# Gate products of a gated recurrence: three single-pass products with halves made by GpSimd, in place of one four-pass product with a VectorE copy

## The chip, the cores and the metric

One NeuronCore of one Trainium2 chip runs the whole program. The time is the device time of one execution in microseconds (us), the median of several runs. Engines are named as in the profile: PE is TensorE's matmul side, PEld its weight load, DVE is VectorE, ACT is ScalarE, POOL is GpSimd, SP is SyncE (it issues most DMAs). SBUF is the on-chip memory of the engines, PSUM the accumulators that PE writes.

## The reference, cut to what matters

One layer of a decoder for 256 prompt tokens and 64 sample tokens (8 sequences of 8), width 1024, all in fp32:

```python
proj = x @ w_in + b_in                                # 1024 -> 7 x 1024: xa, ga, b_gate, c_gate, v, m_a, m_b
xa_c = causal_dwconv(xa, ...)  + conv_a_b             # width 4
r = sigmoid(blockdiag(wa) xa_c + ba)                  # 16 heads of 64 x 64: the gate products
i = sigmoid(blockdiag(wx) xa_c + bx)
a = exp(-8 r softplus(-lam));  b = sqrt(1 - a^2) * (i * xa_c)
h = scan(h = a h + b)
y_a = h * gelu(ga);  y_b = b_gate * causal_dwconv(c_gate * v, ...)
x = layernorm(alpha x + (sigmoid(m_a) y_a + sigmoid(m_b) y_b) @ w_out)
x = layernorm(alpha x + moe_ffn(x))                   # 32 experts, 4 of them for each token, fp32 weights
```

The change touches the two gate products (`r` and `i`) alone.

## The kernel before, in words

**Stages.** First the projection: 8 blocks c of 128 channels, each with 7 pieces of `w_in` (xa, c_gate, v, ga, b_gate, m_a, m_b, called j = 0 to 6; q = 7c + j counts them to 55). Then the product with `w_out`, layer norm and routing, then 32 experts (with a few extra rounds), whose weights SP streams through a ring of 11 slots of 2 MB. This stream of some 400 MB begins to fill slots when the projection is over: a slot is loaded when PE has signalled that its last content was read, and the first slots when `proj_done`, `block_ok`, `first_free`, `wout_done` and the end of the layer norm say so.

**A piece of the projection.** SP loads `raw` (128 x 8 x 128 fp32, 512 KB). ACT writes its high half `w_hi` (L484, type fp32r, which PE multiplies in one pass), DVE writes `w_lo = raw - w_hi` (L1067, called from `split_low(q)`, signal `lo_ok`), and PE does 24 matmuls of 128 x 320 (L712): w_hi x_hi, w_hi x_lo, w_lo x_hi for each of 8 slices of the inner dimension. PE may begin piece q when `lo_ok` is q + 1 and ACT has taken the PSUM bank. There are four buffers each of raw, w_hi and w_lo.

**Order on DVE, written out by hand.** In block c DVE does: the copy of the two 128 x 128 gate weights of the block, `wab` to `wcur` (L1139); a copy of conv state (L1142); `w_lo` of j = 4; the convolution of xa into `xc` (L1145, L1146, then six L1110), which signals `xc_ok`; three small copies (L1153 to L1156); `w_lo` of j = 5; the products and the convolution of c_gate v (L1159 to L1167); `w_lo` of j = 6 and of the next block's j = 0, 1, 2; then the work on the gates, which begins with what ACT made of them, has `w_lo` of the next block's j = 3 in its midst, a reciprocal (L1187) and the scan (L1196), and ends with `mixT` (L1200). After most steps DVE waits for its own semaphore (`link`).

**The gates.** After piece j = 6 PE waits for `wcur_ok`, `xc_ok` and the two PSUM banks, and does two products (L722), one with each 128 x 128 weight, of plain fp32 with 320 columns. ACT takes both results (L534, L536), applies tanh (L539), loads a table and takes a square root (L541), and then makes the w_hi of the next block's j = 3.

```python
pe.wait_ge(wcur_ok, c + 1); pe.wait_ge(xc_ok, c + 1); pe.wait_ge(gates_taken, 2 * c + 2)
for a in range(2):
    mm(PS[:, 6 + a, 0:T], wcur[:, a, :], xc, start=True, stop=True).then_inc(gates_done, 1)
```

**POOL** makes constants at the start, zeroes `wab` (its blocks off the diagonal; SP loads the rest behind that), and does nothing after 4 us. `wab` lies in rows 0 and 1 of `x1`, and row 2 holds the raw state rows until PE has turned them (`st_turned`).

Of the kernel before, what the change touches and what calls it, by code (L numbers as in the profile page):

```python
# [13 lines left out]
P = 128  # L14
D = 1024
KC = D // P
SEQ, DB, DS = 256, 8, 8
NS = DB * DS
T = SEQ + NS
# [26 lines left out]
ALU = mybir.AluOpType  # L46
ACT = mybir.ActivationFunctionType
AX_X = mybir.AxisListType.X
F32 = mybir.dt.float32
F32R = mybir.dt.float32r  # L50
I32 = mybir.dt.int32
U32 = mybir.dt.uint32
ds = bass.ds
# [25 lines left out]
def hybrid_layer(nc, x_prompt, x_sample, state_h, state_conv, state_sc, w_in, b_in, conv_a_w,  # L79
# [5 lines left out]
    with ctx:  # L85
# [3 lines left out]
        def sem(name):  # L89
            return ctx.enter_context(nc.semaphore(name))  # L90
# [5 lines left out]
        slot = 4 * WIDE  # L96
        XT, X1 = SLOTS * slot, SLOTS * slot + 12 * D
# [4 lines left out]
        def place(name, shape, offset, dt=F32):  # L102
            return nc.alloc_sbuf_tensor_at(name, shape, dt, offset=base + offset)
# [37 lines left out]
        wab = x1[:, 0:2, :].rearrange("p a (c n) -> p a c n", c=KC)  # L141
# [38 lines left out]
        PS = ctx.enter_context(nc.psum_tensor("PS", [P, 8, HALF], F32))  # L180


        tiles = place("tiles", [P, 12 * T + 2 * P], 5 * slot)
        bgt, cgt, vt, gel, tma, tmb, xc, tr, ti, rr, aa, sq = (tiles[:, i * T:(i + 1) * T] for i in range(12))
        wcur = tiles[:, 12 * T:12 * T + 2 * P].rearrange("p (a n) -> p a n", a=2)
        hh = vt
        uc = cgt
        xa_p, xa_s = xa_pad[:, 0:259], xa_pad[:, 259:347].rearrange("p (b s) -> p b s", b=DB)
# [33 lines left out]
        def route(n):  # L222
# [17 lines left out]
        prm_in, st_in, wab_in, misc_in, ln_in = (sem(n) for n in  # L240
                                                 ("prm_in", "st_in", "wab_in", "misc_in", "ln_in"))
# [8 lines left out]
        x_turned, prm_turned, st_turned = sem("x_turned"), sem("prm_turned"), sem("st_turned")  # L250
        proj_done, proj_taken = sem("proj_done"), sem("proj_taken")
        gates_done, gates_taken = sem("gates_done"), sem("gates_taken")
        wcur_ok = sem("wcur_ok")
        prm_ok = sem("prm_ok")
        xa_free, cv_free, xc_ok, block_ok = sem("xa_free"), sem("cv_free"), sem("xc_ok"), sem("block_ok")
        t_ok, sq_ok = sem("t_ok"), sem("sq_ok")
# [202 lines left out]
        def _(pool):  # L459
# [13 lines left out]
            pool.iota(row_no[:, :], pattern=[[0, 1]], base=0, channel_multiplier=1,  # L473
                      allow_small_or_imprecise_dtypes=True).then_inc(const_ok, 1)


        @block.scalar
        def _(act):
# [25 lines left out]
            for q in range(NP):  # L504
                c, j = q // 7, q % 7
# [45 lines left out]
                act.activation(xT[:, :, t0:t0 + n], src, ACT.Copy).then_inc(x1T_ok, 1)  # L551


            act.wait_ge(wcur_ok, KC)
            act.wait_ge(block_ok, HALF_K + 1)
            for t in range(2):
                act.activation(mix_s[:, t, 0], mix_of(t), ACT.Copy).then_inc(mixhi_ok, 1)
# [6 lines left out]
            for q, t in enumerate(T_ORDER):  # L564
                n = TILES[t][1]
# [5 lines left out]
            t0, n = TILES[T_ORDER[2]]  # L571
# [75 lines left out]
            for q, (t, _) in enumerate(LAST_SUMS):  # L647
                n = TILES[t][1]
# [11 lines left out]
        def _(pe):  # L660
            mm = pe.matmul
# [29 lines left out]
            def turn_rows():  # L691

                pe.wait_ge(prm_in, 112)
                pe.transpose(PS[:, 6, 0:BIN], vrows[0:BIN, 0, :], ident[0:BIN, 0:BIN])
                pe.transpose(PS[:, 6, BIN:NPRM], vrows[0:7 * KC, 1, :], ident[0:7 * KC, 0:7 * KC])\
                  .then_inc(prm_turned, 1)
                pe.wait_ge(st_in, 48)
                for k in range(KC):
                    last = pe.transpose(PS[:, 7, k * 48:(k + 1) * 48], st_rows[0:48, k * P:(k + 1) * P],
                                        ident[0:48, 0:48])  # L700
                last.then_inc(st_turned, 1)

            for q in range(NP):
                c, j = q // 7, q % 7
                pe.wait_ge(lo_ok, q + 1)
                if q > 0:
                    pe.wait_ge(proj_taken, 7 * c + {0: 8, 6: 9}.get(j, j + 2))
                for k in range(KC):
                    if q == 0:
                        pe.wait_ge(xlo_ok, k + 1)  # L710
                    for n, (w, x) in enumerate(((w_hi, x_hi), (w_hi, x_lo), (w_lo, x_hi))):
                        last = mm(PS[:, j % 6, 0:T], w[:, q % RING, k, :], x[:, k, :],  # L712
                                  start=(k == 0 and n == 0), stop=(k == KC - 1 and n == 2))
                last.then_inc(proj_done, 1)
                if q == 0:
                    turn_rows()
                if j == 6:
                    pe.wait_ge(wcur_ok, c + 1)
                    pe.wait_ge(xc_ok, c + 1)
                    pe.wait_ge(gates_taken, 2 * c + 2)  # L720
                    for a in range(2):
                        mm(PS[:, 6 + a, 0:T], wcur[:, a, :], xc, start=True, stop=True).then_inc(gates_done, 1)  # L722

# [1 line left out]
            def project(t, a, ks):  # L727

                t0, n = TILES[t]
                out = PS[64 * a:64 * a + n, 4, :] if t == 2 else PS[0:n, 2 * t + a, :]  # L730
                first, final = {2: (0, KC - 1), 0: (HALF_K, -1), 1: (-1, KC - 1)}[t]
                for k in ks:
                    last = mm(out, mixT[:, k, t0:t0 + n], out_rows(k // 2)[:, k % 2, a * HALF:(a + 1) * HALF],  # L733
                              start=(k == first), stop=(k == final))
                return last
# [11 lines left out]
            for k in range(KC - 1):  # L747
                pe.wait_ge(block_ok, k + 2)
                pe.wait_ge(wout_in[k // 2], 16)
                for a in range(2):  # L750
                    last = project(2, a, [k])
# [4 lines left out]
            for a in range(2):  # L756
                last = project(2, a, [KC - 1])
# [7 lines left out]
            for a in range(2):  # L765
                last = project_split(1, a)
# [41 lines left out]
            for k in range(KC):  # L808
                last = pe.transpose(PS[0:54, 6 + k // 4, (k % 4) * P:(k % 4 + 1) * P], so[:, k, :], ident[:, :])
# [6 lines left out]
               start=False, stop=False)  # L816
            mm(PS[:, 5, 2 * NE:3 * NE], ones_r[:, :], mask[:, 0, :], start=False, stop=True).then_inc(rank_done, 1)
            for t in range(3):
                last = mm(PS[:, 4, 3 * NE:4 * NE], ones_r[:, :], mask[:, t, :], start=(t == 0), stop=(t == 2))
# [186 lines left out]
            i, n, twice = NE - 1, UNITS * (NE - 2), 2 * n_more  # L1006
# [27 lines left out]
            for u in range(2):  # L1034
                w = ring[:, (n + 10 + u) % SLOTS, :]
                for half in range(2):
                    pe.wait_ge(last_in[2 * u + half], 16)
                    last = down(w, hT_last, u, (2 * half, 2 * half + 1), 1)
# [9 lines left out]
            for a in range(2):  # L1048
                pe.wait_ge(ylo_ok, 2 * n_more + (NE + a))
                for t, bank in LAST_SUMS:  # L1050
                    t0, n = TILES[t]
                    last = mm(PS[0:n, bank + a, :], onehotT[:, 1, t0:t0 + n], ys[:, a, :], start=True, stop=True)
# [5 lines left out]
        def _(dve):  # L1058
# [50 lines left out]
            def stt(out, in0, scalar, in1, op0, op1):  # L1109
                return dve.scalar_tensor_tensor(out=out, in0=in0, scalar=scalar, in1=in1, op0=op0, op1=op1)  # L1110
# [6 lines left out]
                part = bias4[rows, c - 1, :]  # L1117
                return dve.tensor_tensor(part, bias_raw[rows, (c - 1) * HALF:c * HALF], part.bitcast(F32), ALU.subtract)

            dve.wait_ge(wab_in, 64)  # L1120
            for c in range(KC):
                def ahead(j):
                    if 7 * c + j < NP:
# [11 lines left out]
                def by_seq(ap, j):  # L1135
                    return ap.rearrange("p (b j) -> p b j", j=j)


                dve.tensor_copy(wcur[:, :, :], wab[:, :, ds(c, 1), :].rearrange("p a c n -> p (a c) n"))\  # L1139
                   .then_inc(wcur_ok, 1)  # L1140

                link(dve.tensor_copy(xa_s[:, :, 0:3], by_seq(state(8, 24), 3)))  # L1142
                ahead(4)
# [3 lines left out]
                for j in range(1, 4):  # L1147
                    stt(pr(xc), xa_p[:, j:j + SEQ], par(CAW + 8 * j, c), pr(xc), ALU.mult, ALU.add)
                    last = stt(sm(xc), xa_s[:, :, j:j + DS], par(CAW + 8 * j, c), sm(xc), ALU.mult, ALU.add)
# [32 lines left out]
                if 1 <= c <= 3:  # L1182
                    last = bias_low(c, 1)
# [57 lines left out]
            for q, t in enumerate(T_ORDER):  # L1241
                n = TILES[t][1]
# [29 lines left out]
            for q, t in enumerate(T_ORDER):  # L1272
                n = TILES[t][1]
# [6 lines left out]
                last = dve.tensor_tensor(mask[:, t, :], left[:, t, 0:NE], lg[:, t, 0:NE], ALU.is_gt)  # L1280
# [28 lines left out]
            for h in range(2):  # L1309
                last = dve.tensor_copy(pos4[:, :, h, 0, :], posm[:, :, :])  # L1310
# [139 lines left out]
            for q, (t, bank) in enumerate(LAST_SUMS):  # L1450
                n = TILES[t][1]
# [5 lines left out]
            for q, (t, _) in enumerate(LAST_SUMS):  # L1457
                n = TILES[t][1]
# [4 lines left out]
                last = stt(x1[0:n, t, :], y_acc[0:n, t, :], mean[0:n, t:t + 1], ln2g[0:n, :], ALU.add, ALU.mult)  # L1463
# [7 lines left out]
            for q, (t, _) in enumerate(LAST_SUMS):  # L1471
                n = TILES[t][1]
# [27 lines left out]
```

## Time and profile before

| | |
|---|---|
| Time, median of 3 runs | 1194.76 us (1194.38 to 1196.05) |
| The profiled execution | 1195.21 us, span of its instructions 1193.4 us |
| Granted clock of TensorE, mean over the span | 0.992 of full speed |
| PE busy | 1144.0 us (96%) |
| DVE busy | 520.1 us (44%) |
| ACT busy | 259.5 us (22%) |
| POOL busy | 3.3 us, 13 instructions |
| The 8 blocks of the projection | from 12 to 222 us of the span |
| Expert stage | from about 271 us to the end |
| DMA in the expert stage | 424 to 429 GB/s in all slices of the page from 328 us to 1163 us |

Times in the text are positions in the span unless they are called durations. A group of instructions has one row with its count (x4 is four records); a plain fp32 matmul of the gates shows as two records. In the timelines and the chain the first number is the start, the second the duration, both in us. A number in square brackets is idle time of the engine before that instruction, with what ended it. The records of successive matmuls overlap, so the distance between starts, not the duration of one, is what a matmul costs. The chain that ended last goes back from the last instruction to what released each step, so what stands in it set the end of the span.

### The profile page before, as it was taken

To read this page: it belongs to the slowest core of one execution; us is meant where nothing else is said; L and a number is where in the kernel's file an instruction comes from. 1 tells how busy PE (TensorE), PEld (TensorE's weight loads), DVE (VectorE), ACT (ScalarE), POOL (GpSimd) and SP (SyncE) were. 2 spreads that over 40 slices of the span, in tenths; PEclk is the share of its full clock that TensorE was granted. 3 is DMA by queue.
4 is the path that set the end of the run, shared out by engine and by line. 5 is a ranking of instruction groups with operands and counts; after the bars stand their busy time and mean duration, and the time that the engine had idled before them with its cause. 6 is when DMAs were issued, how large, how long until landed. Compare 5 with 4: busy or idle time off the path is not lost.

```text
span 1193.4 us, 13950 instructions
## 1 busy us (share of the span) xinstructions
PE 1144.0 (96%) x5682; PEld 555.5 (47%) x5682; DVE 520.1 (44%) x989; ACT 259.5 (22%) x405; POOL 3.3 (0%) x13
## 2 busy tenths in 40 slices
PE   9999999999999999999999989999999999999994
PEld 8999999663333333333333323333333333333331
DVE  6788788882333222333223332322222222222236
ACT  4655655411111111111111111111111111111112
POOL 1000000000000000000000000000000000000000
PEclk9999999999999999999999999999999999999998
DMA  9866964768999999999999999999999999999994
GB/s 235 256 208 176 265 192 132 289 258 331 416 424 427 428 427 427 428 428 428 427 427 428 428 426 427 428 427 428 427 428 429 426 426 428 429 427 427 426 426 158
DMA packets 93420, 443.77 MB, mean 372 GB/s; under 512 B 7864, under 2 KB 65352, under 8 KB 68014
## 3 DMA queue, kind: packets, MB, share of 16 engines
q1 hardware_dynamic: 93182, 442.41, 92.1%
q8 instruction: 45, 0.74, 0.3%
q10 hardware_dynamic: 176, 0.48, 0.1%
q14 instruction: 17, 0.14, 0.0%
HBM read 441.34 MB, written 1.53 MB: 371 GB/s over the span
## 4 chain that ended last, share of the span: by engine, by line
PE 66%; DMA 24%; DVE 7%; ACT 2%; issue 1%; DVEq 0%; SPq 0%; ACTq 0%
PE PS L921 25%; DMA ring<-in_w_gu 19%; PE PS L961 13%; PE PS L712 10%; PE PS L829 6%; DMA ring<-in_w_down 4%; PE PS L851 3%; PE PS L733 2%; PE PS L837 1%; DVE w_lo L1067 1%; DVE tiles L1110 1%; PE PS L844 1%; PE PS L884 1%; PE PS L743 1%; PE PS L1001 1%
## 5 line engine op out<-in xcount | busy, mean ns | idle before, releaser
L921 PE MATMUL PS<-ring,mid 128*64 128x512 f32 x1920 | 422.0, 593 | 20.7 <-DMA ring<-in_w_gu 20.2
L921 PEld LDWEIGHTS PS<-ring,mid 128*64 128x64 f32 x1920 | 135.8, 137 | 300.1 <-issue 257.9
L961 PE MATMUL PS<-ring,mid 128*64 128x512 f32 x960 | 213.1, 596 | 0.0
L1389 DVE TENSOR_SCALAR PS<-PS 128x512 f32<-128x512 f32 x30 | 21.0, 699 | 353.5 <-PE PS L921 353.5
L712 PE MATMUL PS<-x_hi,w_hi 128*128 128x320 f32 x448 | 141.1, 315 | 1.1 <-ACT tiles L530 0.5
L712 PE MATMUL PS<-x_lo,w_hi 128*128 128x320 f32 x448 | 138.9, 310 | 0.0
L712 PE MATMUL PS<-x_hi,w_lo 128*128 128x320 f32 x448 | 138.9, 310 | 0.0
L1371 DVE TENSOR_TENSOR ys<-PS,ys 64x512 fp32r<-64x512 f32 x64 | 44.1, 689 | 193.9 <-ACT ys L617 185.5
L961 PEld LDWEIGHTS PS<-ring,mid 128*64 128x64 f32 x960 | 66.1, 137 | 130.1 <-issue 130.0
L1110 DVE SCALAR_TENSOR_TENSOR x_tok<-PS,gate,x_tok 128x1024 f32<-128x1024 f32 (+1 forms) x93 | 115.0, 1276 | 20.9 <-PE PS L851 20.9
L608 ACT ACTIVATE mid<-PS 128x512 f32<-128x512 f32 x30 | 17.9, 597 | 419.1 <-DVE PS L1389 419.1
L829 PE MATMUL PS<-x,onehot 128*64 128x512 f32 (+1 forms) x396 | 98.7, 617 | 2.9 <-DVE esel L1288 2.9
L712 PEld LDWEIGHTS PS<-x_hi,w_hi 128*128 128x128 f32 x448 | 84.6, 189 | 4.2 <-DVE w_lo L1067 3.5
L712 PEld LDWEIGHTS PS<-x_lo,w_hi 128*128 128x128 f32 x448 | 84.5, 189 | 0.3
L712 PEld LDWEIGHTS PS<-x_hi,w_lo 128*128 128x128 f32 x448 | 84.5, 189 | 0.0
L617 ACT ACTIVATE ys<-PS 64x512 fp32r<-64x512 f32 x60 | 35.5, 591 | 209.2 <-PE PS L961 208.5
L1067 DVE TENSOR_TENSOR w_lo<-raw,w_hi 128x1024 fp32r<-128x1024 f32 x56 | 67.2, 1222 | 19.5 <-ACT w_hi L484 18.9
L851 PE MATMUL PS<-ys,onehotT 128*128 128x512 f32 (+1 forms) x186 | 64.8, 431 | 0.0
L484 ACT ACTIVATE w_hi<-raw 128x1024 fp32r<-128x1024 f32 x56 | 59.1, 1055 | 18.5 <-DMA raw<-in_w_in 18.4
L829 PEld LDWEIGHTS PS<-x,onehot 128*64 128x64 f32 (+1 forms) x396 | 22.8, 136 | 56.0 <-issue 52.3
L851 PEld LDWEIGHTS PS<-ys,onehotT 128*128 128x128 f32 (+1 forms) x186 | 25.5, 176 | 25.4 <-issue 25.2
L585 ACT ACTIVATE mid<-PS 128x512 f32<-128x512 f32 x33 | 19.7, 597 | 67.6 <-PE PS L829 67.6
(241 smaller groups left out, 750.6 us busy)
## 6 DMA issues: line engine op xcount, KB each, us to landing
ring<-in_w_gu SPq DMA_DIRECT2D x125, 2048.0 KB, 41.9
ring<-in_w_down SPq DMA_DIRECT2D x61, 2048.0 KB, 40.2
raw<-in_w_in SPq DMA_DIRECT2D x56, 512.0 KB, 5.9
ring<-in_w_gu SPq DMA_DIRECT2D x6, 1024.0 KB, 8.6
ring<-in_w_down SPq DMA_DIRECT2D x6, 1024.0 KB, 40.1
ring<-in_w_out SPq DMA_DIRECT2D x4, 1024.0 KB, 5.0
x_tok<-in_x_prompt SPq DMA_DIRECT2D x2, 512.0 KB, 5.2
out<-x SPq DMA_DIRECT2D x2, 512.0 KB, 2.7
```

The lines of the kernel that those rows point to most:

```text
L484: act.activation(w_hi[:, q % RING], raw[:, q % RING], ACT.Copy).then_inc(hi_ok, 1)
L617: act.activation(y_rows(a, 0), PS[64 * a:64 * a + 64, XB, :], ACT.Copy).then_inc(yhi_ok, 1)
L712: last = mm(PS[:, j % 6, 0:T], w[:, q % RING, k, :], x[:, k, :], start=(k == 0 and n == 0), stop=(k == KC - 1 and n == 2))
L733: last = mm(out, mixT[:, k, t0:t0 + n], out_rows(k // 2)[:, k % 2, a * HALF:(a + 1) * HALF], start=(k == first), stop=(k == final))
L829: last = mm(PS[64 * a:64 * a + 64, XB, :], onehot[0:n, t, :], x1[0:n, t, a * HALF:(a + 1) * HALF], start=(t == 0), stop=(t == 2))
L851: last = mm(PS[0:n, bank + a, :], onehotT[:, par, t0:t0 + n], ys[:, a, :], start=True, stop=True)
L921: last = mm(PS[64 * a:64 * a + 64, b, :], xgT[:, 2 * (u % 2) + j, u // 2, :], w[:, o:o + HALF], start=False, stop=(u == 3 and j == 1))
L961: last = mm(PS[64 * a:64 * a + 64, XB, :], hT[:, j, u, :], w[:, j * D + a * HALF:j * D + (a + 1) * HALF], start=(u == 0 and j == 0), stop= ...
L1067: dve.tensor_tensor(w_lo[:, q % RING], raw[:, q % RING], w_hi[:, q % RING].bitcast(F32), ALU.subtract).then_inc(lo_ok, 1)
L1110: return dve.scalar_tensor_tensor(out=out, in0=in0, scalar=scalar, in1=in1, op0=op0, op1=op1)
L1371: last = dve.tensor_tensor(y_rows(a, 1), PS[64 * a:64 * a + 64, bank, :], y_rows(a, 0).bitcast(F32), ALU.subtract)
L1389: dve.tensor_scalar(gm, gm, LIMIT, None, ALU.min).then_inc(gm_ok, 1)
```

## The change

The two gate weights and `xc` are each split into a high half (rounded to fp32r) and a low half (the rest), and each gate product becomes three single-pass products, hi hi, hi lo and lo hi, as the projection does it. The halves are made on POOL: per block a copy and a subtraction of 128 x 256 for the weights, after the gates of the block before have been multiplied, and a copy and a subtraction of 128 x 320 for `xc`, after `xc_ok`. DVE's copy L1139 goes, with its wait for the load of `wab`. The buffers stand where `wcur` was and in row 2 of `x1`. ACT's wait ahead of `mix_s` (which overwrites `wab`) is for POOL's last reading of the weights.

```diff
+        gw_hi = place("gw_hi", [P, 2, P], 5 * slot + 48 * T, F32R)
+        gw_lo = place("gw_lo", [P, 2, P], X1 + 8 * D, F32R)
+        gx_hi = place("gx_hi", [P, T], X1 + 8 * D + 8 * P, F32R)
+        gx_lo = place("gx_lo", [P, T], X1 + 8 * D + 8 * P + 4 * T, F32R)
...
+            pool.wait_ge(wab_in, 64)
+            pool.wait_ge(st_turned, 1)
+            for c in range(KC):
+                if c > 0:
+                    pool.wait_ge(gates_done, 2 * c)
+                pool.tensor_copy(gw_hi[:, :, :], wab[:, :, c, :]).then_inc(pool_gate, 1)
+                pool.wait_ge(pool_gate, 2 * c + 1)
+                pool.tensor_tensor(gw_lo[:, :, :], wab[:, :, c, :], gw_hi[:, :, :].bitcast(F32), ALU.subtract)\
+                    .then_inc(gw_read, 1)
+                pool.wait_ge(xc_ok, c + 1)
+                pool.tensor_copy(gx_hi[:, :], xc).then_inc(pool_gate, 1)
+                pool.wait_ge(pool_gate, 2 * c + 2)
+                pool.tensor_tensor(gx_lo[:, :], xc, gx_hi[:, :].bitcast(F32), ALU.subtract).then_inc(gx_ok, 1)
...
-            act.wait_ge(wcur_ok, KC)
+            act.wait_ge(gw_read, KC)
...
                 if j == 6:
-                    pe.wait_ge(wcur_ok, c + 1)
-                    pe.wait_ge(xc_ok, c + 1)
+                    pe.wait_ge(gw_read, c + 1)
+                    pe.wait_ge(gx_ok, c + 1)
                     pe.wait_ge(gates_taken, 2 * c + 2)
                     for a in range(2):
-                        mm(PS[:, 6 + a, 0:T], wcur[:, a, :], xc, start=True, stop=True).then_inc(gates_done, 1)
+                        for n, (w, x) in enumerate(((gw_hi, gx_hi), (gw_hi, gx_lo), (gw_lo, gx_hi))):
+                            last = mm(PS[:, 6 + a, 0:T], w[:, a, :], x[:, :], start=(n == 0), stop=(n == 2))
+                        last.then_inc(gates_done, 1)
...
-            dve.wait_ge(wab_in, 64)
             for c in range(KC):
...
-                dve.tensor_copy(wcur[:, :, :], wab[:, :, ds(c, 1), :].rearrange("p a c n -> p (a c) n"))\
-                   .then_inc(wcur_ok, 1)
```

## Rows read from the trace of the kernel before

**Rows 1.** Page, part 1: busy time of each engine.

```profile
PE 1144.0 (96%) x5682; PEld 555.5 (47%) x5682; DVE 520.1 (44%) x989; ACT 259.5 (22%) x405; POOL 3.3 (0%) x13
```

**Rows 2.** Stretches: length, busy us per engine, clock, DMA share, GB/s.

```profile
143.00:169.00 26.00, 25.90 (x173) 25.31 (x173) 22.32 (x48) 14.99 (x21) 0.00 (x0) 1.00 0.73 223
...
300.00:600.00 300.00, 300.00 (x1389) 109.63 (x1391) 99.77 (x156) 40.12 (x68) 0.00 (x0) 1.00 1.01 427
```

**Rows 3.** Chain that ended last, 80 to 172: start us, us, what.

```profile
91.29 1.08 PE PS L722 x4
92.37 21.11 PE PS L712 x144
...
117.29 1.08 PE PS L722 x4
...
143.28 1.09 PE PS L722 x4
...
150.01 2.16 DVE tiles L1187
...
165.58 3.79 PE PS L712 x24
169.37 1.09 PE PS L722 x4
```

**Rows 4.** Timeline of PEld near 87 us.

```profile
87.03 0.19 PEld L712 LDWEIGHTS PS<-x_hi,w_lo 128*128 128x128 f32 x1
87.51 0.19 PEld L712 LDWEIGHTS PS<-x_hi,w_hi 128*128 128x128 f32 x1 [0.29 <-DVE w_lo L1067]
```

**Rows 5.** Timeline of PE around one block's gates.

```profile
142.97 0.31 PE L712 MATMUL PS<-x_hi,w_lo 128*128 128x320 f32 x1
143.12 1.24 PE L722 MATMUL PS<-tiles 128*128 128x320 f32 x4
```

**Rows 6.** Timeline of DVE, the sixth block.

```profile
155.82 0.29 DVE L1139 COPY tiles<-x 128x256 f32<-128x256 f32 x1
156.03 0.17 DVE L1142 COPY dsm<-dsm 128x24 f32<-128x24 f32 x1
...
160.31 1.22 DVE L1067 TENSOR_TENSOR w_lo<-raw,w_hi 128x1024 fp32r<-128x1024 f32 x1
161.44 0.42 DVE L1159 TENSOR_TENSOR dsm<-tiles 128x256 f32<-128x256 f32 x1
...
164.30 4.63 DVE L1067 TENSOR_TENSOR w_lo<-raw,w_hi 128x1024 fp32r<-128x1024 f32 x4
```

**Rows 7.** The same timeline of DVE, just after the gates.

```profile
146.12 0.49 DVE L1110 SCALAR_TENSOR_TENSOR tiles<-tiles 128x320 f32<-128x320 f32 x1 [0.69 <-ACT tiles L539]
...
148.86 1.23 DVE L1067 TENSOR_TENSOR w_lo<-raw,w_hi 128x1024 fp32r<-128x1024 f32 x1 [2.02 <-ACT w_hi L484]
```

**Rows 8.** Timelines of POOL and DVE at the start.

```profile
1.06 0.20 POOL L462 MEMSET ones<- 128x128 f32 x1
...
1.60 0.29 POOL L467 TENSOR_SCALAR_AFFINE_SELECT upper<-upper 128x128 f32<-128x128 f32 x1
1.84 1.80 POOL L469 MEMSET x<- 128x2048 f32 x1
...
2.00 1.78 DVE L1071 CAST upper_r<-upper 128x128 fp32r<-128x128 f32 x1 [1.04 <-POOL upper L467]
```

**Rows 9.** Timelines of PEld and DVE, first and second block.

```profile
40.39 0.19 PEld L712 LDWEIGHTS PS<-x_hi,w_hi 128*128 128x128 f32 x1 [0.97 <-DVE w_lo L1067]
...
60.06 3.49 DVE L1067 TENSOR_TENSOR w_lo<-raw,w_hi 128x1024 fp32r<-128x1024 f32 x3
...
61.47 0.19 PEld L712 LDWEIGHTS PS<-x_hi,w_hi 128*128 128x128 f32 x1
```

**Rows 10.** Chain that ended last, after the blocks and late.

```profile
222.61 14.43 PE PS L733 x48
...
822.50 44.69 DMA ring<-in_w_gu
```

More of the change, by code:

```diff
@@ L184, in hybrid_layer @@
         bgt, cgt, vt, gel, tma, tmb, xc, tr, ti, rr, aa, sq = (tiles[:, i * T:(i + 1) * T] for i in range(12))
-        wcur = tiles[:, 12 * T:12 * T + 2 * P].rearrange("p (a n) -> p a n", a=2)
+        gw_hi = place("gw_hi", [P, 2, P], 5 * slot + 48 * T, F32R)
+        gw_lo = place("gw_lo", [P, 2, P], X1 + 8 * D, F32R)
+        gx_hi = place("gx_hi", [P, T], X1 + 8 * D + 8 * P, F32R)
+        gx_lo = place("gx_lo", [P, T], X1 + 8 * D + 8 * P + 4 * T, F32R)
         hh = vt
@@ L252, in hybrid_layer @@
         gates_done, gates_taken = sem("gates_done"), sem("gates_taken")
-        wcur_ok = sem("wcur_ok")
+        gw_read, gx_ok, pool_gate = sem("gw_read"), sem("gx_ok"), sem("pool_gate")
         prm_ok = sem("prm_ok")
```

## The prediction

> **What bounds the kernel now.** I began with the page's busy times: PE is busy for 96% of the span [rows 1]. That says little here, since the stages have different limits, so the table of stretches came next. A block of the projection takes 26 us, with PE busy for 25.9, DVE for 22.3, ACT for 15.0 and DMA at a share of 0.73; the expert stage has DMA at 1.01 and 427 GB/s [rows 2]. So DMA cannot set the pace of a block, and PE and DVE are both near to it. The chain of waits tells which. The gate products recur every 26.00, 25.99 and 26.09 us (91.29, 117.29, 143.28, 169.37) [rows 3], but PE's own work in a block is less: 144 matmuls take 21.11 us, so 0.147 us each, and 168 of them and the gates' 1.08 us make 25.7 [rows 3]. The missing 0.3 us is where one piece begins: PEld's starts are 87.03 and 87.51, 0.48 us apart where 0.147 is usual, and the idle time is ended by DVE's w_lo [rows 4]. That is the piece j = 6, the last before the gates.
>
> So from the third block on a loop through three engines sets the period: gates on PE, tanh and square root and one w_hi on ACT, then a run of DVE work (w_lo, reciprocal at 150.01, scan, mixT, copy L1139, both convolutions and three w_lo), and PE's last piece at 165.58, whose end lets the gates go [rows 3, 6]. The w_lo that this piece waits for is the first of the four from 164.30 on [rows 6]. In that run DVE has no idle time that a row shows: 0.33 us more work on PE in a block would be free, and each 0.1 us more on DVE is 0.1 us of the period. After the blocks PE works through 14.43 us of w_out products without a stall, and much later PE waits for the weight stream [rows 10]. The stream's first slots are released by the end of the projection and what follows it, and it then runs at a constant rate, so I take a shift of the last gates as a shift of the end, one for one.
>
> **The change part by part.**
>
> *Gates on PE.* Removed: four records, 1.08 us a block [rows 3, 5]. Added: six single-pass matmuls of the same 320 columns at 0.147 us, 0.88 us. Gain 0.20 us a block, in the loop. In the first block it is worth nothing: there PE waits 0.97 us for a late w_lo after the gates [rows 9].
>
> *DVE's copy.* Its start is 0.21 us before the next one's [rows 6]. It lies in the loop, so 0.21 us a block. The dropped wait for the load of `wab` had long passed, and the new one stands on POOL, where nothing is queued behind it but the halves themselves.
>
> *Halves of the weights on POOL.* They are due 25 us after POOL may begin, and begin when the gates are done. DVE then has idle stretches of 0.69 and 2.02 us [rows 7], enough for what POOL might hold up there. Cost nothing; without that cover they would cost about as much as the halves of xc.
>
> *Halves of xc on POOL.* For PE they are early: `xc_ok` comes three small copies ahead of the w_lo at 160.31 [rows 6], the gates only at 169.37 [rows 3]. But POOL works exactly in DVE's run without slack. What one does to the other is in the trace once: DVE's CAST of 128 x 128 starts at 2.00, while POOL's memset holds 1.84 to 3.64, and takes 1.78 us, to 3.78 [rows 8]. A DVE copy of twice the columns takes 0.29 [rows 6]. So that instruction stood still until POOL had finished. If DVE's operations in the run do the same, DVE loses about the duration of the two POOL operations in each block; call it d.
>
> How long they are no row shows. Least: the memset goes at (1.80 - 0.20)/1920 = 0.83 ns a column with 0.09 fixed [rows 8], so 0.36 us each for 320 columns, 0.72 together. Most: the affine_select of 128 columns, which reads and writes, 0.29 us [rows 8], scaled by 2.5 to 0.73 for the copy and twice that for the two inputs of the subtraction, 2.2 together. Splitting off the fixed 0.09 gives (0.29 - 0.09)/128 = 1.56 ns a column, 0.59 for the copy, and half as much again for a second input, 0.84: 1.4. Between memset and affine_select a copy is nearer to the latter; some 0.2 goes into the small gaps between DVE's instructions. I take d = 1.2, between 0 (no mutual wait) and 2.2.
>
> The Trainium skill (GPSIMD Engine Reference, Performance versus the Vector engine) has 4497 ns for a two-input addition of 2048 columns, and at best 1.8 cycles of 1.2 GHz a column for a tight loop. By these an estimate would be 0.70 + 0.48 = 1.18; no row here shows either.
>
> *The sum.* In the second block w_lo of j = 6 ends at 61.29 (the first of three from 60.06, 1.23 each) and PE takes it at 61.47 [rows 9]: 0.14 us of room beside 0.04 for the signal, and 0.21 more by the copy. With d = 1.2 PE stalls for 0.85, less 0.20 for the gates: +0.65. The six blocks after it each change by d - 0.21 - 0.20 = +0.79: +4.7. Together +5.4. Against the profiled execution, 1195.21, that is 1200.6; it is 0.45 above the median, so 1200.2 for the median. The change breaks even at d = 0.43.
>
> **Rivals.**
>
> *Only part of DVE's operations wait.* The one case in the trace is a cast from SBUF with one input. The run holds copies and tensor_scalar of that kind, but mostly two-input operations, the w_lo at 160.31 and L1159 at 161.44 first [rows 6]. If these don't wait, only the copies just after `xc_ok` stand still for POOL's first operation, and the second runs beside the 1.22 us of w_lo: d = 0.45, and -0.1 + 6 x 0.04 = +0.1 us, 1194.9. Against it: nothing in the rows, for no two-input DVE operation ran beside POOL. The Trainium skill speaks to it (SBUF — State Buffer, Who interferes with whom): a VectorE instruction with two SBUF inputs contends with a GpSimd one that reads SBUF, and the second to come fully blocks. The cast's row agrees with its rule for copies and casts; by it this rival falls.
>
> *Nothing waits: faster.* d = 0, if the row of the cast is an accident of the start. One mechanism: DVE's run gets 0.21 us shorter and the gates 0.20, so -0.20 in the second block and -0.41 in each of six, 0.12 above what PE's own work allows: -2.7, 1192.1. It decides below d = 0.43. For it: POOL has no other work, and the xc halves have 8 us. Against it: the 1.78 us of the cast.
>
> *POOL comes last.* If DVE's back to back run keeps POOL out, POOL gets its turn when the four w_lo end at 168.93 [rows 6], makes the halves in some 1.3 us and the gates start at 170.2 instead of 169.2. PE then waits at the gates: +1.0 - 0.41 a block, seven blocks, +4.2: 1199.0. Against it: DVE's waits on its own semaphore leave gaps in the run.
>
> **How the numbers follow.** Forecast (d between 0.7 and 2.2) 0.50, POOL last 0.12, only part waits 0.17, nothing waits 0.21. A change of 0.2%, 2.4 us, is about what a measurement can tell from none. The forecast and POOL last are slower: 0.62, with 0.01 of the former left below the bound. Part waits is the same, and so is a fifth of nothing waits, whose -2.7 lies close to the bound: 0.22. Faster: 0.17. The range reaches down to the fast case, 1192.0, just below its centre, and up to d = 1.75, which gives 1.40 - 0.20 + 6 x 1.34 = +9.2, so 1204.0; beyond it lie the last of the bounds (2.2 would be 1.85 - 0.20 + 6 x 1.79 = +12.4, 1207.2) and the lower half of the fast case. Cases of both signs hold much of the chance; the forecast's own range, d from 0.8 to 1.9, is 1197.4 to 1205.
>
> **What the profile afterwards would show.** Right: L722 gives way to 48 matmuls with starts 0.147 apart. POOL has 32 more instructions; those on xc stand at the three small copies of DVE, and one of the DVE records there (a copy, the w_lo of j = 5, or L1159) is longer by about POOL's duration; PEld's idle time before j = 6, 0.29 now, grows to about 1.3 (0.79 of the period and the 0.20 that the gates give), ended by w_lo, and the period from gates to gates is 26.8. POOL's records on the weights make DVE's records after the gates longer without moving the w_lo that waits for ACT. Wrong: DVE's records unchanged and the period 25.6 (nothing waits); PE idle before the gates, ended by POOL (POOL last); a period of 26.8 with PE's stall elsewhere. The expert stage should only be shifted; if the end moves by less than the last gates, my one for one is the wrong step.

## The result, and the profile after

The changed kernel takes 1197.83 us (median of 12 runs, 1196.33 to 1199.2) against 1195.61 us before (12 runs, 1194.38 to 1197.08): 2.2 us more, ratio 1.0019 with a 95% interval of 1.0012 to 1.0027. It is slower: the interval leaves out 1, though the difference is just below the 2.4 us that the prediction took as the least that a measurement can tell. The profiled executions, 1197.42 and 1195.21 us, differ by the same 2.2.

The page of the changed kernel, parts 1 and 4 (the chain that ended last, by engine, then by line). L729 is now the matmul of the pieces, L740 that of the gates, L1086 the w_lo, L1129 the helper for scalar_tensor_tensor, L1177 what was L1162.

```profile
PE 1142.6 (96%) x5698; PEld 556.4 (47%) x5698; DVE 528.4 (44%) x981; ACT 259.6 (22%) x405; POOL 37.8 (3%) x45
...
PE 55%; DMA 28%; DVE 12%; issue 2%; ACT 2%; SPq 1%; DVEq 0%; ACTq 0%
PE PS L940 23%; DMA ring<-in_w_gu 22%; PE PS L980 12%; PE PS L848 6%; DMA ring<-in_w_down 4%; PE PS L870 3%; DVE w_lo L1086 2%; PE PS L729 2%; DVE tiles L1129 2%; PE PS L752 2%; DMA raw<-in_w_in 1%; PE PS L856 1%; DVE tiles L1202 1%; PE PS L863 1%; PE PS L903 1%
```

POOL has gone from 3.3 to 37.8 us of busy time [rows 1], DVE from 520.1 to 528.4 in spite of its dropped copy, and DVE stands in the chain with 12%, where before it had 7% (part 4 of the page of before). The table of stretches has a block so (columns as in [rows 2]):

```profile
144.00:170.00 26.00, 25.41 (x173) 25.09 (x172) 22.60 (x47) 14.89 (x21) 4.22 (x4) 1.00 0.71 218
```

PE is busy for 25.4 us of 26 instead of 25.9. The chain of waits, 80 to 172 us:

```profile
91.47 0.89 PE PS L740 x6
...
117.86 0.89 PE PS L740 x6
...
144.23 0.89 PE PS L740 x6
...
165.61 1.24 DVE w_lo L1086
166.89 3.78 PE PS L729 x24
170.67 0.89 PE PS L740 x6
```

The gates are six records, 0.89 us instead of 1.08, and recur every 26.39, 26.37 and 26.44 us, where [rows 3] has 26.00, 25.99 and 26.09. Their starts on PE are 0.15 us apart, as forecast:

```profile
144.07 0.31 PE L740 MATMUL PS<-gx_hi,gw_hi 128*128 128x320 f32 x1
144.22 0.31 PE L740 MATMUL PS<-gx_lo,gw_hi 128*128 128x320 f32 x1
```

No run here counts the passes of a plain fp32 product. What the traces show is two records and 0.54 us for a plain fp32 product (1.08 for two), and one record and 0.147 us for each product of halves.

PE waits in the same place as before, ahead of the piece j = 6, and for the same thing, but for 0.79 us instead of 0.29 [rows 4]:

```profile
86.71 0.19 PEld L729 LDWEIGHTS PS<-x_hi,w_lo 128*128 128x128 f32 x1
87.68 0.19 PEld L729 LDWEIGHTS PS<-x_hi,w_hi 128*128 128x128 f32 x1 [0.79 <-DVE w_lo L1086]
```

The loop is still closed by DVE's w_lo of j = 6, the first of the four of L1086: it starts at 165.61, and PE's piece at 166.89. So what did DVE do? Its timeline in the sixth block:

```profile
145.96 1.45 DVE L1129 SCALAR_TENSOR_TENSOR tiles<-tiles 128x320 f32<-128x320 f32 x2
...
149.62 1.23 DVE L1086 TENSOR_TENSOR w_lo<-raw,w_hi 128x1024 fp32r<-128x1024 f32 x1 [1.98 <-ACT w_hi L501]
...
160.85 1.22 DVE L1086 TENSOR_TENSOR w_lo<-raw,w_hi 128x1024 fp32r<-128x1024 f32 x1
161.98 0.42 DVE L1174 TENSOR_TENSOR dsm<-tiles 128x256 f32<-128x256 f32 x1
162.32 0.22 DVE L1175 TENSOR_TENSOR dsm<-tiles 128x64 f32<-128x64 f32 x1
162.58 0.42 DVE L1176 TENSOR_SCALAR tiles<-dsm 128x256 f32<-128x256 f32 x1
162.92 0.94 DVE L1177 TENSOR_SCALAR tiles<-dsm 128x64 f32<-128x64 f32 x1
163.90 1.40 DVE L1129 SCALAR_TENSOR_TENSOR tiles<-dsm,tiles 128x256 f32<-128x256 f32 x4
```

and POOL's:

```profile
145.18 0.40 POOL L484 CAST gw_hi<-x 128x256 fp32r<-128x256 f32 x1 [7.80 <-PE PS L740]
145.66 0.87 POOL L486 TENSOR_TENSOR gw_lo<-x,gw_hi 128x256 fp32r<-128x256 f32 x1
160.77 2.08 POOL L489 CAST gx_hi<-tiles 128x320 fp32r<-128x320 f32 x1 [14.25 <-DVE tiles L1129]
162.93 0.88 POOL L491 TENSOR_TENSOR gx_lo<-tiles,gx_hi 128x320 fp32r<-128x320 f32 x1
```

What to see: POOL's cast of xc starts when xc is ready, beside DVE's copies, and its record lasts 2.08 us, to 162.85. Over that time DVE does its w_lo and two more two-input operations in exactly the times of before, 1.22, 0.42 and 0.22 [rows 6 has the first two]: here POOL stands still, not DVE. Only the tensor_scalar of 256 columns behind them is longer, 0.42 instead of 0.35. Then POOL's subtraction runs from 162.93 to 163.81, and DVE's tensor_scalar of 64 columns, 162.92 to 163.86, ends just behind it. In the kernel before, the same place reads

```profile
162.03 0.35 DVE L1161 TENSOR_SCALAR tiles<-dsm 128x256 f32<-128x256 f32 x1
...
162.59 1.40 DVE L1110 SCALAR_TENSOR_TENSOR tiles<-dsm,tiles 128x256 f32<-128x256 f32 x4
```

and the eight records of the second tensor_scalar took (min, median, max in ns)

```profile
L1162 DVE TENSOR_SCALAR tiles<-dsm x8: 248/249/251, 29.7 to 214.5; 128x64 f32<-128x64 f32 x8
```

so it stood still for 0.69 us. From the start of this w_lo to the start of the convolution behind the tensor_scalar, DVE needs 163.90 - 160.85 = 3.05 us; in the kernel before it was 162.59 - 160.31 = 2.28. The difference, 0.77, is the d of the prediction. Only 0.07 of it goes to the cast. POOL's work on the weights does lengthen DVE's records after the gates: in the pair from 145.96 the first scalar_tensor_tensor, an operation with two inputs, lasts 0.92 us instead of 0.49. But the w_lo at 149.62 waits for ACT all the same.

The rest is a shift. PE's first expert work in the chain starts at 273.56, 1.83 us later than before; the last gates end 1.83 later too (224.44 against 222.61, [rows 10]):

```profile
224.44 14.43 PE PS L752 x48
...
273.56 7.09 PE PS L940 x32
```

```profile
271.73 7.09 PE PS L921 x32
```

(the first fence is the changed kernel's chain, the second that of before).

### The profile page after: what moved, and what is told of

The parts are those of the page before. It is cut to its first block, busy times and chain, and to the rows that moved or that the text cites. A ratio compares the mean times of both kernels' runs of the same rounds, so it can differ in the third digit from the quotient of the medians.

```text
span 1195.7 us, 14007 instructions
## 1 busy us (share of the span) xinstructions
PE 1142.6 (96%) x5698; PEld 556.4 (47%) x5698; DVE 528.4 (44%) x981; ACT 259.6 (22%) x405; POOL 37.8 (3%) x45
## 4 chain that ended last, share of the span: by engine, by line
PE 55%; DMA 28%; DVE 12%; issue 2%; ACT 2%; SPq 1%; DVEq 0%; ACTq 0%
PE PS L940 23%; DMA ring<-in_w_gu 22%; PE PS L980 12%; PE PS L848 6%; DMA ring<-in_w_down 4%; PE PS L870 3%; DVE w_lo L1086 2%; PE PS L729 2%; DVE tiles L1129 2%; PE PS L752 2%; DMA raw<-in_w_in 1%; PE PS L856 1%; DVE tiles L1202 1%; PE PS L863 1%; PE PS L903 1%
## 5 line engine op out<-in xcount | busy, mean ns | idle before, releaser
L729 PE MATMUL PS<-x_hi,w_hi 128*128 128x320 f32 x448 | 139.9, 312 | 5.7 <-DVE w_lo L1086 3.8
L729 PE MATMUL PS<-x_hi,w_lo 128*128 128x320 f32 x448 | 138.5, 309 | 0.0
L729 PE MATMUL PS<-x_lo,w_hi 128*128 128x320 f32 x448 | 138.5, 309 | 0.0
L1129 DVE SCALAR_TENSOR_TENSOR x_tok<-PS,gate,x_tok 128x1024 f32<-128x1024 f32 (+1 forms) x93 | 115.0, 1275 | 20.9 <-PE PS L870 20.9
L729 PEld LDWEIGHTS PS<-x_hi,w_hi 128*128 128x128 f32 x448 | 84.1, 188 | 8.4 <-DVE w_lo L1086 7.9
L729 PEld LDWEIGHTS PS<-x_lo,w_hi 128*128 128x128 f32 x448 | 84.1, 188 | 0.0
L729 PEld LDWEIGHTS PS<-x_hi,w_lo 128*128 128x128 f32 x448 | 84.1, 188 | 0.0
L1086 DVE TENSOR_TENSOR w_lo<-raw,w_hi 128x1024 fp32r<-128x1024 f32 x56 | 67.5, 1229 | 17.3 <-ACT w_hi L501 16.6
L870 PEld LDWEIGHTS PS<-ys,onehotT 128*128 128x128 f32 (+1 forms) x186 | 25.5, 176 | 25.4 <-issue 25.1
```

What stands on the lines that cost most here:

```text
L870: last = mm(PS[0:n, bank + a, :], onehotT[:, par, t0:t0 + n], ys[:, a, :], start=True, stop=True)
L1086: dve.tensor_tensor(w_lo[:, q % RING], raw[:, q % RING], w_hi[:, q % RING].bitcast(F32), ALU.subtract).then_inc(lo_ok, 1)
```

## The experiments

All are compared with the kernel before on the same chip. "Last gates" is PEld's first weight load for the last block's gates, "six periods" the time from there back to the second block's gates, which leaves the varying first loads out; both are read from the one profiled execution. The medians of the kernel before beside which the ratios stand are 1195.12 us for e1 to e4, 1195.60 for e5 to e8 and 1195.12 for e9 to e12. Several intervals end close to 1, so the periods carry the argument: those of the third and fourth block agree to 0.02 us in every kernel but e8.

| kernel | period, third and fourth block | six periods | last gates | span | time, median | ratio to before (95%) |
|---|---|---|---|---|---|---|
| before | 26.00, 25.99 | 156.2 | 221.2 | 1193.4 | 1195.61 | |
| changed | 26.37, 26.39 | 158.5 | 223.2 | 1195.7 | 1197.83 | 1.0019 (1.0012, 1.0027) |
| e1 copy out, no POOL | 25.80, 25.80 | 155.0 | 219.8 | 1192.1 | 1194.03 | 0.9990 (0.9981, 0.9999) |
| e2 no low half of xc | 25.67, 25.67 | 154.2 | 218.9 | 1190.8 | 1193.35 | 0.9987 (0.9977, 0.9997) |
| e3 copy back | 26.57, 26.58 | 159.7 | 225.3 | 1196.9 | 1198.46 | 1.0028 (1.0018, 1.0038) |
| e5 POOL alone | 26.59, 26.58 | 159.7 | 224.7 | 1197.2 | 1199.06 | 1.0032 (1.0020, 1.0044) |
| e11 second cast | 25.94, 25.92 | 155.8 | 220.3 | 1193.0 | 1194.72, one | |
| e12 no weight halves | 26.38, 26.37 | 158.5 | 223.5 | 1194.7 | 1196.50, one | |
| e4 behind w_lo, DVE waits | 25.83, 25.83 | 155.4 | 220.2 | 1192.3 | 1194.35 | 0.9999 (0.9989, 1.0008) |
| e6 behind w_lo | 25.61, 25.59 | 154.4 | 219.1 | 1190.7 | 1192.73, one | |
| e10 the same, timed | 25.62, 25.63 | 154.5 | 220.4 | 1192.2 | 1193.87 | 0.9988 (0.9979, 0.9997) |
| e7 ACT high, POOL low | 25.62, 25.61 | 154.8 | 220.7 | 1192.2 | 1195.77 | 1.0002 (0.9993, 1.0011) |
| e8 one w_lo later | 25.61, 25.83 | 155.2 | 219.1 | 1191.4 | 1194.91 | 0.9997 (0.9988, 1.0006) |
| e9 later bias wait | 25.62, 25.61 | 153.9 | 219.1 | 1190.6 | 1192.98 | 0.9988 (0.9979, 0.9998) |

Span less last gates lies between 971.2 and 972.6 in all fourteen, while the last gates move by 6.4 us. So the stages behind pass a shift on one for one, and add some 0.7 us either way of their own.

**e1, the copy alone.** Expected:

> The kernel before with one part of the change alone: DVE's copy L1139 is left out and PE reads the gate weights where they lie, in plain fp32; no work on POOL. Theory (the period of a block is set by a loop through PE, ACT and DVE, and DVE's run has no slack): the period from gates to gates falls by the copy's 0.21 us, from 26.0 to 25.8, in six blocks, and the second block has nothing to win; 1.3 us faster than before, 1194.3. Rival (DVE's copy lies beside other work): the period stays 26.0 and the time 1195.6.

```diff
-                        mm(PS[:, 6 + a, 0:T], wcur[:, a, :], xc, start=True, stop=True).then_inc(gates_done, 1)
+                        mm(PS[:, 6 + a, 0:T], wab[:, a, c, :], xc, start=True, stop=True).then_inc(gates_done, 1)
-                dve.tensor_copy(wcur[:, :, :], ...).then_inc(wcur_ok, 1)
```

Its chain:

```profile
90.93 1.08 PE PS L720 x4
...
116.73 1.08 PE PS L720 x4
```

25.80 us apart: the copy was worth its 0.20 us a block, 1.2 us in six, and the time is 1.1 under the 1195.12 that the kernel before took beside it. The weights could be multiplied where they lay; nothing needed the copy.

**e2, without POOL's subtraction for xc.**

> The changed kernel without POOL's subtraction for xc: the second product of each gate takes the high half of xc again, so PE does the same six matmuls (the low part of xc is left out of the gates). Theory (that subtraction alone holds DVE up, by 0.69 us at the tensor_scalar of 64 columns, while POOL's cast of 2.08 us mostly waits for DVE): the tensor_scalar is back at 0.25 us, the period falls from 26.4 to 25.7, and the time is 2.2 us below the kernel before, 1193.4. Rival (the long cast is what costs, or the wait of PE for POOL): the period stays at 26.3 or more and the time within 1 us of the changed kernel's 1197.8.

```diff
-                pool.tensor_copy(gx_hi[:, :], xc).then_inc(pool_gate, 1)
-                pool.wait_ge(pool_gate, 2 * c + 2)
-                pool.tensor_tensor(gx_lo[:, :], xc, ..., ALU.subtract).then_inc(gx_ok, 1)
+                pool.tensor_copy(gx_hi[:, :], xc).then_inc(gx_ok, 1)
```

DVE's two tensor_scalar:

```profile
160.35 0.42 DVE L1173 TENSOR_SCALAR tiles<-dsm 128x256 f32<-128x256 f32 x1
160.69 0.25 DVE L1174 TENSOR_SCALAR tiles<-dsm 128x64 f32<-128x64 f32 x1
```

The second is back at 0.25, the first is still at 0.42. The period is 25.67: the cast is there, with its record of 2.08 us, and still all but 0.07 of the loss is gone and both gains of the change show (26.00 - 0.20 - 0.20 + 0.07). The rival, the long cast, falls.

**e3, DVE's copy back in.**

> The changed kernel with DVE's copy of 128 x 256 back at its old place, its result unused. Theory (DVE's run sets the period): 0.21 us more in each of seven blocks, period 26.6, 1.5 us over the changed kernel, 1199.3. Rival (something other than DVE's run sets the new period): no change, 1197.8.

```diff
+                dve.tensor_copy(spare[:, :, :], wab[:, :, ds(c, 1), :]...).then_inc(spare_ok, 1)
                 link(dve.tensor_copy(xa_s[:, :, 0:3], by_seq(state(8, 24), 3)))
```

The period is 26.57, so 0.20 more than in the changed kernel in each block, and 1.2 in six periods; the time is 3.3 over before, against 2.2 for the changed kernel. DVE's run sets the new period too.

**e5, POOL's work on xc alone,** with plain fp32 gates and no copy (e1) and the halves unused.

> The kernel of e1 (no DVE copy, plain fp32 gates, 1194.0) with POOL's cast and subtraction of xc added after xc_ok, their results unused but waited for by the gates. Theory (POOL's two operations cost DVE's run 0.77 us, whatever PE does): period 25.8 + 0.77 = 26.6 in six blocks, 0.4 in the second, so 5.0 us over e1, 1199.0. Rival (the cost belongs to the six matmuls or to reading the halves on PE): near e1, 1194.0.

```diff
+                pool.wait_ge(xc_ok, c + 1)
+                pool.tensor_copy(gx_hi[:, :], xc).then_inc(pool_gate, 1)
+                pool.wait_ge(pool_gate, c + 1)
+                pool.tensor_tensor(gx_lo[:, :], xc, ..., ALU.subtract).then_inc(gx_ok, 1)
```

The period is 26.58, 0.78 over e1 (25.80): d measured by itself, with PE's matmuls as they were. So the cost belongs to POOL beside DVE and not to anything on PE. Each against its own kernel before, the times are 3.5 over (e5) and 1.1 under (e1), so 4.6 apart, as the six periods are 4.7 apart; the forecast had 5.0.

**e11, a cast in place of the subtraction.**

> The changed kernel with POOL's subtraction for xc replaced by a second cast (the low part is thereby wrong data: the high half of xc stands in its place). Theory (DVE's tensor_scalar stands still for as long as POOL's second operation lasts, whatever it is): the cast alone takes 0.45 us against 0.88, so the tensor_scalar falls from 0.94 to about 0.5 us and the period from 26.4 to 26.0. Rival (only a two-input operation on POOL holds DVE up): tensor_scalar 0.25, period 25.7.

```diff
-                pool.tensor_tensor(gx_lo[:, :], xc, gx_hi[:, :].bitcast(F32), ALU.subtract).then_inc(gx_ok, 1)
+                pool.tensor_copy(gx_lo[:, :], xc).then_inc(gx_ok, 1)
```

DVE's two tensor_scalar, then POOL's two casts:

```profile
160.97 0.42 DVE L1176 TENSOR_SCALAR tiles<-dsm 128x256 f32<-128x256 f32 x1
161.31 0.49 DVE L1177 TENSOR_SCALAR tiles<-dsm 128x64 f32<-128x64 f32 x1
```

```profile
159.16 2.08 POOL L489 CAST gx_hi<-tiles 128x320 fp32r<-128x320 f32 x1 [14.25 <-DVE tiles L1129]
161.31 0.46 POOL L491 CAST gx_lo<-tiles 128x320 fp32r<-128x320 f32 x1
```

POOL's second operation has halved, 0.46 instead of 0.88, and so has what the tensor_scalar loses: 0.49 - 0.25 = 0.24 instead of 0.69. The period is 25.93. So DVE's loss follows the duration of POOL's operation and is no fixed price. It is about 0.2 us less than that duration both times (0.88 - 0.69, 0.46 - 0.24).

**e12, the weights' halves for the first block only.**

> The changed kernel with the halves of the gate weights made for the first block only (the later blocks multiply with those; their own weights are left out). Theory (POOL's work on the weights is hidden in DVE's idle time after the gates): period 26.4 as in the changed kernel, sum of the seven unchanged within 0.2 but for the start. Rival (it costs too): period lower, by up to 0.3.

```diff
-                pool.tensor_copy(gw_hi[:, :, :], wab[:, :, c, :]).then_inc(pool_gate, 1)
+                if c == 0:
+                    pool.tensor_copy(gw_hi[:, :, :], wab[:, :, c, :]).then_inc(pool_gate, 1)
...
-                    pe.wait_ge(gw_read, c + 1)
+                    pe.wait_ge(gw_read, 1)
```

DVE, just after the gates of the fifth block:

```profile
147.11 0.49 DVE L1130 SCALAR_TENSOR_TENSOR tiles<-tiles 128x320 f32<-128x320 f32 x1 [0.50 <-ACT tiles L557]
...
149.85 1.22 DVE L1087 TENSOR_TENSOR w_lo<-raw,w_hi 128x1024 fp32r<-128x1024 f32 x1 [2.02 <-ACT w_hi L502]
```

DVE's records there are short again, and its idle time before the w_lo is 2.02 us as in [rows 7]; the six periods are 158.5 as in the changed kernel. This part of POOL's work costs nothing, as the prediction had it.

**e4, POOL's work on xc behind the w_lo of j = 6, and DVE waiting for it.**

> The changed kernel with POOL's two operations on xc moved behind the w_lo of j = 6, and DVE waiting for them before its next three w_lo, which have over 3 us of slack. Theory (POOL and DVE exclude each other, and only what precedes the w_lo of j = 6 counts): POOL's cast falls from 2.08 to about 0.5 us, the tensor_scalar is back at 0.25, the gates find their halves some 2 us early, the period is 25.6, and the time 2.7 us below the kernel before, 1192.9. Rival (the halves are then too late for the gates, or DVE's later work on the gates is pushed into the loop): PE idle before the gates or a longer wait of ACT's and DVE's after them, period 26.0 or more.

```diff
                 pool.wait_ge(xc_ok, c + 1)
+                pool.wait_ge(lo_ok, 7 * c + 7)
...
-                for j in range(6, 10):
+                ahead(6)
+                dve.wait_ge(gx_ok, c + 1)
+                for j in range(7, 10):
                     ahead(j)
```

```profile
165.49 0.45 POOL L490 CAST gx_hi<-tiles 128x320 fp32r<-128x320 f32 x1 [19.53 <-DVE w_lo L1087]
166.02 0.88 POOL L492 TENSOR_TENSOR gx_lo<-tiles,gx_hi 128x320 fp32r<-128x320 f32 x1
```

Undisturbed, the cast takes 0.45 and the subtraction 0.88 us. The last three periods are 25.67, but the two of the table are 25.83 and the one from the fourth to the fifth block's gates 26.78, so that the six sum to 155.4 instead of 154.0, and the time cannot be told from before. Half a miss, then. The two are blocks in which DVE also prepares the expert bias; that its wait of 1.6 us pushes this into the loop is a reading, which e7 bears out. In the 26.78 ACT waits for a load, and SP issues it late:

```profile
129.23 1.06 ACT L502 ACTIVATE w_hi<-raw 128x1024 fp32r<-128x1024 f32 x1 [6.64 <-DMA raw<-in_w_in]
```

```profile
104.87 8.43 SPq L333 DMA_DIRECT2D raw<-in_w_in  x3
122.29 0.37 SPq L390 DMA_DIRECT2D ring<-in_w_out  x1
122.70 6.32 SPq L333 DMA_DIRECT2D raw<-in_w_in  x4
```

(first ACT's w_hi, then SP's issues.) SP has nothing to do between 113.3 and 122.29: it stands at its wait for that bias, ahead of a load of w_out, and the pieces' loads queue behind it. The kernel before does the same, 0.7 us earlier (the w_out load at 121.60), and has just enough time.

**e6 and e10, the same without DVE's wait.**

> e4 without DVE's wait: POOL may begin on xc when the w_lo of j = 6 is done, while DVE goes on with three more. Theory (whichever has the port keeps the other out, and DVE's next instruction comes before POOL's): POOL's cast is held until the run of w_lo ends, some 3.5 us long instead of 0.45, the halves come after PE is ready, and PE idles about 1.2 us before the gates: period 26.6 or more. Rival (POOL gets in between two w_lo): cast about 1.5 us, no idle before the gates, period 25.7.

```profile
164.29 1.31 POOL L490 CAST gx_hi<-tiles 128x320 fp32r<-128x320 f32 x1 [19.59 <-DVE w_lo L1087]
165.69 1.74 POOL L492 TENSOR_TENSOR gx_lo<-tiles,gx_hi 128x320 fp32r<-128x320 f32 x1
```

```profile
162.94 5.57 DVE L1087 TENSOR_TENSOR w_lo<-raw,w_hi 128x1024 fp32r<-128x1024 f32 x4
```

The theory's forecast for this one was wrong. The cast takes 1.31 and the subtraction 1.74 us: POOL waits for about one w_lo each time and then gets in, and DVE's four w_lo take 5.57 instead of 4.63 us [rows 6], 0.94 more: the third lasts 1.47 and the fourth 1.90 instead of 1.22. For PE the delay falls on w_lo that have over 3 us of slack. The subtraction ends at 167.43, the gates start at 167.69, 0.26 us later, and PE does not wait for them. The period is 25.6, but for the fifth block's, 26.17. It also shows that a w_lo, with its two inputs, does stand still for POOL, as the scalar_tensor_tensor after the gates does in the changed kernel, while in the run before j = 6 POOL waited for all of them. Timed:

> The kernel of e6 again, timed. The gates' seven periods add up to 154.4 us there, 1.8 less than in the kernel before (156.2) and 4.0 less than in the changed one (158.5). Theory (a shift of the last gates is a shift of the end): 1.8 us faster than before, 1193.7, and about 4 faster than the changed kernel. Rival (the single 1192.7 of e6 was its start or its stream): no difference from before that can be measured.

(What is called seven periods there are the six between seven gates.) 1193.87 against 1195.12, ratio 0.9988 (0.9979 to 0.9997): faster than both kernels, by the one added line. The slow fifth block is in part still POOL's doing. The chain of e10 there:

```profile
112.43 5.58 DVE w_lo L1087 x4
...
122.32 0.37 SPq L390
122.73 6.61 DMA raw<-in_w_in
```

DVE's work on the bias stands behind the four lengthened w_lo, SP waits for it, and the late load follows.

**e7 and e8, two ways to shorten DVE's wait in e4.**

> e4 with the high half of xc made by ACT, in its idle time before the piece j = 5, so that behind the w_lo of j = 6 POOL has the subtraction alone and DVE waits 1.0 us instead of 1.6. Theory: the period is 25.67 in all blocks, also in those with bias work (25.83 in e4), and the fifth block loses less than e4's 1.1 us to a late load; 2.4 to 2.7 us faster than before, 1192.6. Rival (ACT's extra 0.5 us comes into the loop, or the late load stays): as e4 or slower, 1194.3.

> e4 with POOL's work on xc and DVE's wait one w_lo later, so that the w_lo of the next block's j = 0 is not held. Theory: the halves are ready 0.5 us before the gates, the w_lo that the loads wait for come earlier, and the fifth block loses less than in e4; the blocks with bias work stay at 25.83: 1193.3. Rival (the load is late because DVE's bias work is, which this does not change): the fifth block at 26.8 as in e4, 1194.3.

```diff
 e7:
+                if j == 5:
+                    act.wait_ge(xc_ok, c + 1)
+                    act.activation(gx_hi[:, :], xc, ACT.Copy).then_inc(gxh_ok, 1)
 e8:
+                pool.wait_ge(lo_ok, min(7 * c + 8, NP))
```

In their profiles the six periods are 154.8 and 155.2. In e7 the bias blocks are back at 25.62, as expected, and the late block costs 0.7 us; in e8 it costs 1.0, nearly as in e4, as its rival had it. Their medians, 1195.77 and 1194.91, are 0.2 us over and 0.7 under before and can't be told from it. For e7 that is 1.6 us worse than its six periods promise (154.8 - 156.2 = -1.4). Its runs spread from 1193.3 to 1198.9, and only one of them has a profile, so why stays open.

**e9, e6 with SP's bias wait two places later.**

> e6 with SP's wait for the bias, and the loads of w_out behind it, two places later in SP's queue, and the two loads of slot 10 in their place. Theory (in the fifth block the w_hi wait for loads that SP issues late, since it stands at the bias wait): the fifth block's period falls from 26.2 to 25.7, the sum of the periods from 154.4 to 153.9, 0.5 us under e6. Rival (the loads are late by their own bandwidth): no change, or the late block moves to the seventh.

```diff
-                    if k == 6:
+                    if k == KC:
                         sp.wait_ge(bias_ok, 1)
                     if k < 6:
                         load_half(k // 2, k % 2)
                     elif k < KC:
-                        load_out(k - 6)
+                        load_half(10, k - 6)
                     else:
-                        load_half(10, k - KC)
+                        load_out(k - KC)
```

SP's issues, then the chain:

```profile
114.08 9.62 SPq L333 DMA_DIRECT2D raw<-in_w_in  x4
123.74 0.58 SPq L354 DMA_DIRECT2D ring<-in_w_down  x1
```

```profile
by line: PE PS L730 90.7%; PE PS L753 5.8%; PE PS L741 3.6%
...
116.76 0.88 PE PS L741 x6
...
142.37 0.88 PE PS L741 x6
```

SP no longer stands still ahead of the fifth block's loads, the fifth block's period is 25.61, the six sum to 153.9, and the chain runs through PE alone: 90.7% in the pieces' matmuls. The time is 1192.98, ratio 0.9988 (0.9979 to 0.9998). The 0.5 us between e9 and e6 shows in the profile, and is too small for the timed runs.

## Why the prediction was right, and where its size was off

*What bounds a block.* Right: the loop through gates, ACT, DVE's run and the piece j = 6. DVE's 0.2 us came off the period in e1 and went onto it in e3 to within 0.01 us.

*Gates on PE.* Right: 0.20 forecast, 1.08 - 0.88. It came off the period: e5, with plain fp32 gates and no halves of the weights, has 26.58, and the changed kernel, with the same work of POOL on xc, 26.38.

*DVE's copy.* Right: 0.21 forecast, 0.20 in e1.

*Halves of the weights.* Right: nothing (e12).

*Halves of xc.* The mechanism was right: POOL and DVE exclude each other, in the run without slack. The step that failed is the size of its term, "DVE loses about the duration of the two POOL operations": I took 1.2 and it is 0.77. The durations were good (0.59 and 0.84 forecast, 0.45 and 0.88 measured in e4). What was wrong is that both fall on DVE. The cast waited for three two-input operations of DVE in a row and cost DVE 0.07 us; only the subtraction held DVE up, for 0.69 of its 0.88. The 0.2 that I took off once is right, but it comes off each operation: in e6, where both fall on DVE, they cost 0.94 of 1.33. The one case in the trace of before had POOL first, and I took both operations to go that way.

*The sum.* With 0.77 in the prediction's own formula: second block 0.77 - 0.35 = 0.42 of stall, less 0.20; then 6 x (0.77 - 0.41) = 2.2; together 2.4. The profile has 158.5 - 156.2 = 2.3 in the six periods, and the timed runs have 2.2. The forecast of +5.4 was 2.4 times too much, and no run stands at the break-even of 0.43. On its two sides, the changed kernel with 0.77 is slower, and e11 with 0.31 (26.00 - 0.41 + 0.31 = 25.90) has a period of 25.93 and six periods of 155.8 against 156.2.

*The number.* That 1197.83 lies in the range, 1192.0 to 1204.0, says little, since the range took in a faster kernel as well as a slower one. It even lies just within the forecast's own range, d from 0.8 to 1.9, with a d of 0.77, because the kernel before came out at 1195.61 this time and not at the 1194.76 to which the sum was added. That part is luck. The direction, slower, rests on the mechanism.

*Rivals.* "Only part of DVE's operations wait" gave d = 0.45 with the first operation on the wrong side: in fact the tensor_scalar waited for the second, and in e6 the two-input w_lo waited as well. "Nothing waits" is what e2 shows without the subtraction, and its 25.6 is close to the period there, 25.67. It fails for the subtraction. "POOL comes last" did not occur, not even in e6.

*One for one.* Right, to about 0.7 us either way.

The Trainium skill (SBUF — State Buffer, Who interferes with whom) says that a VectorE instruction with two SBUF inputs contends with a GpSimd instruction that reads SBUF, that copies and tensor_scalar in their two-port mode contend with GpSimd too, and that whoever issues first keeps the shared ports for its whole instruction, while the other stands still. The traces agree in both directions: the cast's 2.08 us against 0.45, the tensor_scalar's 0.94 against 0.25, the w_lo run's 5.57 against 4.63. VectorE's loss is about 0.2 us short of a whole GpSimd instruction in each. That the first to issue wins can't be read off the records: the changed kernel's cast starts at 160.77, before the w_lo at 160.85, and ends after it. The same skill's GPSIMD Engine Reference (Performance versus the Vector engine) gave estimates of 0.70 for the subtraction and 0.48 for the cast; e4 has 0.88 and 0.45.

## What to carry to other kernels

Before work is moved to GpSimd, ask not only whether it is done in time but what VectorE does in that moment: in a stretch of VectorE without slack its operations can cost as much there as on VectorE itself (0.77 us here for a copy of 0.21 removed). The same work behind the w_lo of j = 6, the last that PE waits for before the gates, cost nothing in most blocks and about 0.5 us in one: one wait turned 2.2 us lost into 1.3 won. And look first whether a copy is needed at all; leaving it out alone (e1, 1.1 us) was worth about as much as the whole change with that wait (e10, 1.3 us).

## What the runs showed of the hardware that was not expected

- GpSimd waited through three back to back VectorE instructions (w_lo and two tensor_tensor, 1.7 us) when they followed on small copies, but in a row of four w_lo each of its two operations got in after about one (1.31 and 1.74 us for operations of 0.45 and 0.88). What decides between the two was not tried.
- The record of a GpSimd instruction includes its wait: the same cast of 128 x 320 is 0.45 us and 2.08 us. The busy time of POOL, 37.8 us, is therefore no measure of its work. In the same way the tensor_scalar of 64 columns reads 0.25 or 0.94.
- VectorE lost about 0.2 us less than the GpSimd operation lasted: 0.69 of 0.88 (changed kernel), 0.24 of 0.46 (e11), 0.94 of 0.45 and 0.88 together (e6). Why was not tried.
